# Three of four row pairs of each down-projection group as seven products, the first straight behind the up-projection strip, and the strip drained two banks at a time

## The reference

```
h = layer_norm(ALPHA * h + mix_out, ln1_g, ln1_b)
ff = jnp.square(jax.nn.relu(jnp.einsum('bsd,df->bsf', h, mlp_w1) + mlp_b1))
ff_out = jnp.einsum('bsf,fd->bsd', ff, mlp_w2) + mlp_b2
h = layer_norm(ALPHA * h + ff_out, ln2_g, ln2_b)
```

## Time and profile before

| | us |
|---|---|
| median of 3 runs | 2603.95 (2603.46 to 2604.62) |
| the profiled execution: its own time | 2602.97 |
| its span, first to last instruction | 2601.2 |

### The profile page before, as it was taken

How to read it: one execution, slowest core, us unless ns; L and a number is a source line. 1 busy time by engine, 2 the same in 40 slices (tenths; PEclk the granted TensorE clock), 3 DMA queues, 4 the chain that set the end, 5 groups by cost and what they waited for, 6 DMA issues and landing times.

```text
span 2601.2 us, 38339 instructions
## 1 busy us (share of the span) xinstructions
PE 2583.3 (99%) x13264; PEld 2193.8 (84%) x13264; DVE 2028.0 (78%) x2154; ACT 1487.2 (57%) x1731; POOL 43.2 (2%) x32
## 2 busy tenths in 40 slices
PE   9999999999999999999999999999999999999999
PEld 8888888888888888888888888878988888888888
DVE  7787877444445657788787888897679999999997
ACT  6677675344444555556555645577565555555554
POOL 0000000000000100000000002000010000000000
PEclk9999999999999999999999999999999999999999
DMA  7555556555555555665665554544556666665664
GB/s 269 181 185 183 186 192 201 184 190 194 194 197 199 165 191 184 195 204 190 202 200 196 198 193 161 180 141 138 170 177 201 197 202 200 201 202 194 201 201 163
DMA packets 133900, 494.25 MB, mean 190 GB/s; under 512 B 14864, under 2 KB 15376, under 8 KB 133776
## 3 DMA queue, kind: packets, MB, share of 16 engines
q1 hardware_dynamic: 133776, 492.62, 57.3%
HBM read 490.46 MB, written 2.10 MB: 189 GB/s over the span
## 4 chain that ended last, share of the span: by engine, by line
PE 92%; DVE 4%; ACT 2%; issue 2%; DMA 0%; DVEq 0%; SPq 0%; ACTq 0%
PE ps_b L501 14%; PE ps_b L513 7%; PE ps_a L611 5%; PE ps_a L612 5%; PE ps_a L613 5%; PE ps_a L501 5%; PE ps_b L611 4%; PE ps_b L613 4%; PE ps_b L612 4%; PE ps_a L1026 3%; PE ps_a L1028 3%; PE ps_a L1027 3%; PE ps_a L513 3%; PE ps_a L768 2%; PE ps_a L770 2%; PE ps_a L769 2%
## 5 line engine op out<-in xcount | busy, mean ns | idle before, releaser
L1161 ACT ACTIVATE w_hi<-w_raw 128x1024 fp32r<-128x1024 f32 (+1 forms) x908 | 969.2, 1074 | 949.5 <-PE ps_a L613 211.9
L1758 DVE TENSOR_TENSOR w_lo<-w_raw,w_hi 128x1024 fp32r<-128x1024 f32 (+1 forms) x908 | 1118.8, 1249 | 472.3 <-ACT w_hi L1161 467.4
L501 PE MATMUL ps_b<-xx,w_hi 128*128 128x512 f32 x1632 | 398.0, 392 | 3.1 <-ACT w_hi L1161 1.4
L501 PEld LDWEIGHTS ps_b<-xx,w_hi 128*128 128x128 f32 x1632 | 298.0, 188 | 61.9 <-ACT w_hi L1161 2.6
L513 PEld LDWEIGHTS ps_b<-xx,w_lo 128*128 128x128 f32 x1632 | 211.7, 191 | 9.0
L513 PE MATMUL ps_b<-xx,w_lo 128*128 128x256 f32 x1632 | 215.5, 283 | 0.0
L501 PE MATMUL ps_a<-xx,w_hi 128*128 128x512 f32 x672 | 163.7, 391 | 0.0
L501 PEld LDWEIGHTS ps_a<-xx,w_hi 128*128 128x128 f32 x672 | 122.6, 188 | 23.1
L1026 PE MATMUL ps_a<-w_hi,ff 128*128 128x512 f32 x320 | 125.4, 392 | 0.0
L1028 PE MATMUL ps_a<-w_hi,ff 128*128 128x512 f32 x320 | 124.6, 389 | 0.0
L1027 PE MATMUL ps_a<-w_lo,ff 128*128 128x512 f32 x320 | 124.5, 389 | 0.0
(11 more groups left out here) (475 smaller groups left out, 4841.0 us busy)
## 6 DMA issues: line engine op xcount, KB each, us to landing
w_raw<-w_dram SPq DMA_DIRECT2D x836, 512.0 KB, 3.4
w_raw<-w_dram SPq DMA_DIRECT2D x72, 640.0 KB, 4.0
zz<-x_dram SPq DMA_DIRECT2D x8, 256.0 KB, 4.8
x_res<-x_dram SPq DMA_DIRECT2D x4, 512.0 KB, 4.6
out_dram<-res SPq DMA_DIRECT2D x3, 512.0 KB, 2.6
out_dram<-res SPq DMA_DIRECT2D x4, 128.0 KB, 1.8
const<-const_dram SPq DMA_DIRECT2D x1, 449.0 KB, 4.7
prm<-prm_dram SPq DMA_DIRECT2D x1, 308.0 KB, 6.0
```

Of the source, the lines that this page charges most:

```text
L501: last = nc.tensor.matmul(group[:, j, :], w_hi[:, r, o * P:o * P + P], moving(src, at + k), start=begins and k == 0 and not opened, stop=n ...
L1161: act.activation(w_hi[:, r, 0:width], w_raw[:, r, 0:width], ACT.Copy).then_inc(hi_done, 1)
L1758: dve.tensor_tensor(w_lo[:, r, 0:width], w_raw[:, r, 0:width], w_hi[:, r, 0:width].bitcast(F32), ALU.subtract).then_inc(lo_even if r % 2 = ...
```

## The change

In each of the 13 groups pair 0 also goes through seven products (`seven_main_first`), straight behind the strip. Its products into GA (m2, m3, m4) come first, because GB still holds the strip. Then it waits for the first two banks of the strip (`up_first`), does m1 and m5, waits for all four banks (`strip_out`) and does m6 and m7. Pair 3 stays plain. The second and third `seven_products` follow, with the third's weight sums in the buffer that the first used. The strip is drained in two halves: two copies on ACT (`half_first`, `half_out`) and two additions on DVE. Sums of `ff` tiles are made for three pairs (384 columns instead of 256), in a tensor of their own, and their third part has its own rounding on ACT and DVE. In `mixed_in` the next `lo` comes ahead of the wait and scaling. Counters (`n`) are renumbered.

```diff
+            def seven_main_first(done, q, m, first_two, last_two):
+                piece_ready(q, 0)
+                product(m["m2"], True, False)
+                piece_ready(q, 1)
+                product(m["m3"], True, False)
+                pe.wait_ge(t_hi, done + 1)
+                pe.wait_ge(t_lo, done + 1)
+                product(m["m4"], True, False)
+                first_two()
+                product(m["m1"], True, False).then_inc(pe_piece, 1)
+                product(m["m5"], True, False).then_inc(pe_piece, 1)
+                last_two()
+                product(m["m6"], True, False)
+                product(m["m7"], True, False).then_inc(t_used, 1)
...
             def grouped(i, pair, q):
-                for nn in range(2):
-                    pe.wait_ge(acc_out, 2 * n - 1 + nn)
-                    token_pieces([(q, nn, two_tiles(0))], sums_of(nn), ff, 8, need)
-                pe.wait_ge(strip_out, outs(E_MLP + 2 * i + 3 + pair))
+                need(0)
+                pe.wait_ge(acc_out, 2 * n)
                 pe.wait_ge(s_hi, i + 1)
                 pe.wait_ge(s_lo, i + 1)
-                seven_products(True, False, 2 * n - 2, q, 2, product_operands(ff, sums_of_ff(0), 2, 0, 2, GA, GB, thi, tlo))
+                seven_main_first(3 * n - 3, q, product_operands(ff, sums_of_ff(0), 0, buf, 0, GA, GB, thi, tlo),
+                                 lambda: pe.wait_ge(up_first, n),
+                                 lambda: pe.wait_ge(strip_out, outs(E_MLP + 2 * i + 3 + pair)))
+                seven_products(False, False, 3 * n - 2, q, 2, product_operands(ff, sums_of_ff(1), 2, 1 - buf, 2, GA, GB, thi, tlo))
                 need(4)
-                seven_products(False, True, 2 * n - 1, q + 1, 0, product_operands(ff, sums_of_ff(1), 4, 1, 0, GA, GB, thi, tlo))
+                seven_products(False, True, 3 * n - 1, q + 1, 0, product_operands(ff, sums_of_ff(2), 4, buf, 0, GA, GB, thi, tlo))
...
# ScalarE
-            def strip_end(q, e, k, sums, n):
-                splits(q + 2, N8, (0, 1))
-                split_group(n, q + 2, 2)
+            def strip_end(q, e, sums, n, buf):
+                split_group(n, q + 2, 0)
+                t_high(n, buf)
+                t_high(n + 1, 1 - buf)
+                split(q + 2, 2)
                 if sums is not None:
                     act.wait_ge(s_lo, sums + 1)
-                halves(e, 4 * q + 8, GB)
-                t_high(n, 0)
+                act.wait_ge(pe_piece, 4 * q + 8)
+                act.wait_ge(strip_out, outs(e))
+                act.activation(half[:, 0:2, :], GB[:, 0:2, S:2 * S], ACT.Copy).then_inc(half_first, 1)
+                act.activation(half[:, 2:4, :], GB[:, 2:4, S:2 * S], ACT.Copy).then_inc(half_out, 1)
...
# VectorE
-            def strip_end(q, i, k, n):
+            def strip_end(q, i, k, n, count, buf):
+                two_more(0, buf, two_sums(n, q + 2, 0, buf))
                 los(q + 2, N8, (0, 1))
-                two_more(2, 0, two_sums(n, q + 2, 2, 0))
+                t_low(n, buf)
+                two_more(2, 1 - buf, two_sums(n + 1, q + 2, 2, 1 - buf))
+                t_low(n + 1, 1 - buf)
+                dve.wait_ge(half_first, count)
+                dve.tensor_tensor(hid[:, k, 0:2, :], GB[:, 0:2, 0:S], half[:, 0:2, :], ALU.add).then_inc(up_first, 1)
+                dve.wait_ge(half_out, E_MLP + 2 * i + k + 1)
+                dve.tensor_tensor(hid[:, k, 2:4, :], GB[:, 2:4, 0:S], half[:, 2:4, :], ALU.add).then_inc(strip_out, 1)
                 lo(q + 2, 2)
-                two_sums(n + 1, q + 3, 0, 1)
-                summed_strip(E_MLP + 2 * i + k, k, GB)
-                lo(q + 2, 3)
-                t_low(n, 0)
-            def group_end(q, pair, n, done):
-                two_more(0, 1, None)
+            def group_end(q, pair, n, done, buf):
+                lo(q, 3)
+                two_more(0, buf, two_sums(n + 2, q + 1, 0, buf))
                 los(q + 1, N8, (0, 1))
-                t_low(n + 1, 1)
+                t_low(n + 2, buf)
...
             def mixed_in(b, banks):
+                lo(157 + b, 3 - 3 * b)
                 dve.wait_ge(strip_out, outs(E_MIX + b + 1))
                 gained_lo(x2, b, 4 * XX_N2, "n2_g")
```

More of the change, by code:

```diff
@@ L249, in build @@
         x2_raw, ff_turned = sem("x2_raw"), sem("ff_turned")
+        half_first, up_first = sem("half_first"), sem("up_first")
         tile_done, tile_out = sem("tile_done"), sem("tile_out")
@@ L757, in turn_seed, with plain_pieces @@
                 last.then_inc(seed_turned, 1)
+            def plain_pieces(q, r, src, k, bank, first, last):
+                piece_ready(q, r)
+                for n in range(2):
+                    cols = slice(512 * n, 512 * n + 512)
+                    hi, lo = w_hi[:, r, cols], w_lo[:, r, cols]
+                    for t in range(2):
+                        x_hi, x_lo = src[:, k + n, t * P:t * P + P], src[:, k + n, S + t * P:S + t * P + P]
+                        nc.tensor.matmul(bank[:, t, :], x_hi, hi, start=first[t] and n == 0, stop=False)
+                        nc.tensor.matmul(bank[:, t, :], x_hi, lo, start=False, stop=False)
+                        done = nc.tensor.matmul(bank[:, t, :], x_lo, hi, start=False, stop=last and n == 1)
+                done.then_inc(pe_piece, 1)
             def two_tiles(k):
@@ L1016, in need_n2 @@
                     pe.wait_ge(xx_lo, 4 * XX_N2 + k // 4 + 1)
[L1018 to L1029, removed]
             every, none = (True, True), (False, False)
@@ L1446, in squared, with group_end @@
                 act.activation(hid[:, k, :, :], hid[:, k, :, :], ACT.Square).then_inc(ff_made, 1)
-            def group_end(q, i, k, n):
-                split_group(n + 1, q + 1, 0)
-                t_high(n + 1, 1)
+            def group_end(q, i, k, n, buf):
+                split(q, 3)
+                split_group(n + 2, q + 1, 0)
+                t_high(n + 2, buf)
                 splits(q + 1, N8, (2, 3))
@@ L1727, in _ @@
             silu(GA[:, 0:2, :])
[L1728 removed]
+            act.wait_ge(t1_made, 40)
             split(165, 3)
[L1730 to L1731 removed]
+            t_high(39, 0, f_hi, f_raw)
+            split_group(40, 166, 0)
             ff_high_of(0, 0, GA[:, 2:4, :])
[L1733 removed]
+            t_high(40, 1, f_hi, f_raw)
             splits(166, N8, (2, 3))
[L1735 removed]
+            rest(1, 165, 41, 0, 1)
             with act.Fori(0, 4) as c:
                 for k in range(2):
[L1738 removed]
+                    i, q, n = 2 * c + k + 2, 12 * c + 6 * k + 171, 10 * c + 5 * k + 43
                     first_sevens_high(q, n, k)
                     rest(i, q, n + 3, 1 - k, k)
[L1741 to L1742 removed]
+            first_sevens_high(219, 83, 0)
+            rest(10, 219, 86, 1, 0)
             splits(225)
@@ L2226, in next_inputs_of @@
                 dve.wait_ge(ff_made, 2 * i + 2)
-                activation_sums(pairs[:, 1:3, :, :, :], s_sum).then_inc(s_made, 1)
+                activation_sums(pairs[:, 0:3, :, :, :], s_sum).then_inc(s_made, 1)
                 ff_low(ff, i, 0)
@@ L2269, in mlp @@
             def mlp(i, between=None):
[L2271 to L2272 removed]
+                q = 8 * i + 80
+                group_end(q, 0, 6 * i - 3, 2 * i - 1, 1)
                 if between is not None:
@@ L2505, in mixed_in @@
                 dve.wait_ge(pe_piece, 4 * Q0 + MIX_END - 1 + b)
-                dve.tensor_tensor(tiles, banks.rearrange("p b (j s) -> p (b j) s", j=2), tiles, ALU.add).then_inc(strip_out, 1)
+                dve.tensor_tensor(tiles, as_features(banks), tiles, ALU.add).then_inc(strip_out, 1)
+                narrow.append(E_MIX + b)
+                lo(157 + b, 3 - 3 * b)
                 dve.wait_ge(strip_out, outs(E_MIX + b + 1))
                 gained_lo(x2, b, 4 * XX_N2, "n2_g")
-                narrow.append(E_MIX + b)
             for m in range(MIX_END):
@@ L2647, in _ @@
             los(166, N8, (0, 1))
-            t_low(27, 1, f_lo, f_raw, f_hi)
+            t_low(40, 1, f_lo, f_raw, f_hi)
             los(166, N8, (2, 3))
             dve.wait_ge(q_zero, 2)
-            rest(1, 165, 28, 0, 1)
+            rest(1, 165, 41, 0, 1)
             with dve.Fori(0, 4) as c:
@@ L2658, in _ @@
                 own.leave(4)
-            first_sevens_low(219, 70, 0)
-            rest(10, 219, 73, 1, 0)
+            first_sevens_low(219, 83, 0)
+            rest(10, 219, 86, 1, 0)
             lo(225, 0)
```

81 lines of the change are left out of this document (38 added, 43 removed).

## The result

The changed kernel takes **2684.62 us** (median of 4 runs, 2680.87 to 2686.58) against 2604.28 (2603.46 to 2605.58) for the kernel before on the same chip: ratio 1.0303, 95% interval 1.029 to 1.0316, slower. The direction and the new wait behind each strip were as predicted, the size wasn't. The predicted time was 2654 and its range ended at 2680, so 4.6 us of the result lie outside. The profiled execution took 2686.58 us, its span 2684.8.

A forecast was written before the change was run, and what follows sets the result against it. TensorE, busy 99% of the span, was taken as the bound. Terms -8.84 - 0.96 + 6 x 3.5 + 7 x 5.5 = +49.7 us on the profiled 2602.97 gave 2652.7, as median 2654; range 2639 to 2680.

The forecast's parts named there:

- The removal, -8.84 us: In each of 13 groups TensorE loses 3 matmuls of 0.227 us: 0.68 us a group, 8.84 us in all.
- The new wait in an ordinary group, 3.5 us: In six groups TensorE waits 3.5 us before m1 for VectorE's addition, queued behind the second set's `tlo`.
- The long waits, 5.5 us: In seven groups, VectorE late from `next_inputs_of` or combining accumulators: TensorE waits 5.5 us before m1, bounds 5.0 and 6.0.
- The third set, m6 and m7, the second product: Later needs in each group: no further TensorE waits; for the third set 0, upper bound 0.5 us a group.
- `mixed_in`, -0.96: In `mixed_in`, TensorE's wait for a `lo` behind the scaling goes: 0.96 us gained, other bound 0.
- The clock: TensorE's clock after the 13 new waits: 0 in the sum, upper bound 24 us from 1.8 us per restart.
- what stands beside them: A few us added to the range for what stands beside the dissolved backlog and the clock's full price.
- Drain in time: Rival: `up_first` comes within 2.04 us of the strip's end, all gain stays, 2594 us; 3%.
- no change: Rival: no measurable change, with waits of only 0.8 us a group; 2%.
- The backlog dissolves: Rival: TensorE's waits give VectorE time, so all 13 groups cost 3.5 us, 2640 us; 15%.
- VectorE is the bound: Rival: VectorE, at 97%, bounds throughout; 0.5 us more in each group, third set late, 2661 us; 10%.
- The clock falls after each wait: Rival: the clock falls behind each wait, up to 2677 us, or 2667 behind the seven long ones alone; 30%.

The follow-up runs named there:

- experiment 2: The changed kernel with the strip's additions (and ScalarE's copies) ahead of the second set's t3, `t_high` and `t_low`: 2652.02 us, ratio 1.0184.
- experiment 3: The kernel before with only the edit in `mixed_in`: 2604.18 us, ratio 0.9994.
- Experiment 1: The changed kernel with twelve matmuls of zeros added between m4 and the wait for the strip's first two banks: 2670.0 us, ratio 1.0254.
- Experiments 5: The kernel before with 52 one-column memsets on VectorE ahead of its loop over the second block's MLP: 2615.34 us, ratio 1.004.
- experiment 6: The changed kernel with the early additions of experiment 2 and 40 one-column memsets on VectorE ahead of the second block's loop: 2639.89 us, ratio 1.0137.
- experiment 7: Experiment 2 with VectorE's `lo` of slot 3 behind the strip making 2 columns instead of 1024 in each group: 2637.78 us, ratio 1.0129.

## Why the prediction was wrong in its size and right in its direction

- **The removal, -8.84 us: consistent.** The trace has 39 matmuls fewer at the same pace, and the MLP's sum closes with it to 0.4 us. It wasn't measured alone.
- **The new wait in an ordinary group, 3.5 us: right.** 3.22 us in the list, 3.4 by starts (1109.08 - 1105.47 less one pace). The steps came as worked out, as times behind the strip's end: `tlo` of the second set +3.00 (predicted +3.1), addition +4.68 (+4.8), m1 +5.42 (+5.5). VectorE idles 1.55 us on `thi` (predicted about 1.5).
- **The long waits, 5.5 us: near in size, for another reason than predicted in six of seven.** They are 4.7 to 5.5 us, mean 4.9. All waits together were predicted at 59.5 us and measure 56.0. The prediction had t1 wait for the landing of a piece that a late `lo` had let in, and start 6.05 us ahead of the strip's end. In six groups t1 starts 5.8 to 6.4 us ahead of it, but straight behind VectorE's own `lo` (timeline ahead of 1157.01), without a wait for a landing; only in the last group does it wait for one, 3.80 us. That both ways give nearly the same time is luck, and the 0.3 us added for landings stands on nothing.
- **The third set, m6 and m7, the second product: 0 was right** as long as the first wait is that long. With `up_first` in time (experiment 2) 21.9 us of waits appear, 1.7 us a group, at the second product's pieces, which the prediction had at "nothing, within a few tenths"; but there more of VectorE's work stands ahead of that `lo` than in the predicted kernel.
- **`mixed_in`, -0.96: right in the trace**, where the wait is gone, and too small for the medians of experiment 3 to show.
- **The clock: this is the step that failed.** The sum put it at 0, "being nearest to rows 3", though rows 3 reach only to 1.8 us and the sum itself made waits of 3.5 and 5.5. Measured: eight falls in the MLP (granted 0.51 and 0.62 in the windows behind two of them), one behind each of the seven long waits and one behind the first ordinary one, 21.4 us. The row of the start of the program also mispriced a single fall: there 8 starts come at the slow pace, behind a long wait in the MLP it is 11 to 14. The upper bound of 24 came out nearly right only because 13 restarts at 1.8 us are about as much as seven at 2.8 and one at 1.7. Experiment 1 shows the cause: with m1 at the same place and TensorE busy for part of the wait, 14.6 us come back.
- **The second block: a term that the prediction didn't have.** +11.3 us, three stalls of VectorE of up to 3.7 us (10.3 in all) with 15 more instruction fetches, 64 against 49. TensorE loses 1.7 of the 11.3 us to one more fall of the clock, at 2466.00. Experiments 5 and 6 show the cause. The few us that the range kept above 2677 for "what stands beside them" were too few for this term and the next.
- **Small jumps, 4.0 us: not in the prediction either.** They are a few tenths each and weren't followed further.

With what was measured in place of these terms, against the profiled execution: 2652.7 - 3.5 (waits) + 0.4 (`mixed_in` and what lies around it, -0.6 for -0.96) + 21.4 (clock) + 4.0 + 11.3 (second block) = 2686.3, and it took 2686.58. Either of the two large terms alone would have stayed inside the range.

**The rivals.** *Drain in time* and *no change* fell at once. *The backlog dissolves* (2640) fell: long waits stayed 1.7 us longer than ordinary ones. *VectorE is the bound* (2661) fell as priced: 84% busy, and idle 1.55 us in every group right ahead of the wait. Its amount of work does count once the additions come early (experiment 7). *The clock falls after each wait* was the nearest. It had 30%, its top was 2677, and measured it is 8 falls of 13.

The Trainium skill's page "TensorE: Matmul & The Clock Gate" (section "What's actually happening") says that an idle array returns to 1.2 GHz and must be busy again to leave it; by that rule the time would have been up to the 2677 of the rival. The trace agrees for the seven waits of 4.7 us and more, each followed by starts 0.43 us apart. Its section "HAM oscillation — how this bites in real kernels" describes a kernel that pays this anew with every gap; the trace agrees for each second group (2.4 to 3.0 us each time), and not for five of the six ordinary waits of 3.2 us.

**What the slowdown is made of**, then, over the kernel before: the place of the additions in two in-order queues, about 34 us with the clock that falls by it (MLP of experiment 2 against the changed one, 1573.92 and 1607.81); the waits that experiment 2 still has, 46 us over the MLP by starts (31 in jumps over 0.3 us, 15 in smaller ones), of which experiment 7 takes back 14 with 1 us less work for VectorE a group; the place of a loop in the code, 11 to 12 us; against them the 8.84 us gained. How the rest of the 46 us divides between VectorE, ScalarE and the loads wasn't tried. Experiments 6 and 7 weren't combined. Their gains have different causes (the code's place, work in the MLP), and if they add, it would be about 2626, still above 2604.

## What to carry to other kernels

Before a product is put straight behind a strip that must be drained, list what stands ahead of that drain in the draining engine's in-order queue, and what each of those waits for in turn: here the addition needed 0.7 us and came 4.7 us after the strip. If the sum makes the critical engine idle for longer than any wait that the trace of before shows, the price of a clock fall belongs in the sum, since "nothing seen" holds at best for waits as short as those seen (and, by experiment 3, for one of those only in that execution). And when instructions are added ahead of a loop on another engine, look at that engine's idle time "issue" and the number of instruction fetches, even in stages that the change doesn't touch.

## What the runs showed of the hardware

- **Behind a wait of 4.7 us or more the clock fell each time; behind one of 1.8 to 3.3 us it fell sometimes.** Seven of seven waits from 4.7 to 5.5 us brought a fall. Of the six ordinary ones five (3.2 us) left the clock at 1.00 and the first (3.3 us) didn't. Of experiment 1's seven waits of 2.2 to 2.9 us, behind filler of zeros, three brought one. At 2466.00 of the changed kernel a wait of 1.86 us for `f_acc` was enough. And the wait of 1.8 us for `probs`, at the same place of the same code, left the clock up in the kernel before and not in experiment 3. So the length of the wait alone doesn't decide in this range, and one trace without a fall doesn't show that there will be none. What else enters wasn't tried.
- **Where a loop lies in an engine's code can cost 11 us here.** 32 instructions ahead of it changed nothing (49 fetches), 52 cost 11.0 us (65 fetches), 40 in experiment 6 took away 12.1 us (64 fetches to 50). The loop's body has 272 instructions on VectorE. In the slow cases five fetches come in each of three passes, four of them around the return; in the fast ones there is none. That the loop then no longer fits in what is held near the engine is my reading; the runs show only the fetches, the stall of 3.7 us and that moving the code makes and removes it.
